# HGRN intra-chunk products by chunk, two tiles to a bank, the neighbour level without an exponential, and eight weight splits on DVE

## The reference, cut to what matters

```python
CHUNK = 64
def step(state, inp):                       # one chunk of 64 tokens
    q_i, k_i, i_i, b_i = inp                # b_i: running sum of log f inside the chunk
    dmat = jnp.exp(jnp.where(causal, b_i[:, :, :, None, :] - b_i[:, :, None, :, :], -jnp.inf))
    attn = jnp.einsum('bhtk,bhsk,bhtsk->bhts', q_i, k_i, dmat)
    o = (jnp.einsum('bhtk,bhkv->bhtv', q_i * jnp.exp(b_i), state)
         + jnp.einsum('bhts,bhsv->bhtv', attn, i_i))
    state = (state * jnp.exp(b_last[:, :, 0, :])[..., None]
             + jnp.einsum('bhsk,bhsv->bhkv', k_i * jnp.exp(b_last - b_i), i_i))
```

## Time and profile before

| | us |
|---|---|
| median of the runs | 1397.89 |
| span of the profiled execution | 1397.8 |
| PE busy in it | 1207.0 |
| DVE busy in it | 753.0 |
| HGRN stage, first product of `hdiag` to first of `hscan` | 329.6 to 422.0 |

### The profile page before, as it was taken

One profiled execution on the slowest core, in us unless ns is written; L12 is line 12 of the kernel. 1 busy time (PEld: TensorE's weight loads), 2 busy tenths in 40 slices (PEclk: granted clock), 3 DMA queues, 4 the chain that ended last, 5 costly groups with the idle time before them and its releaser, 6 DMA issues.

```text
span 1397.8 us, 17492 instructions
## 1 busy us (share of the span) xinstructions
PE 1207.0 (86%) x5935; PEld 983.9 (70%) x5935; DVE 753.0 (54%) x981; ACT 645.5 (46%) x898; POOL 459.8 (33%) x383
## 2 busy tenths in 40 slices
PE   3995899999789965999939999999998995699990
PEld 2775898888678844878828877888777883578770
DVE  4345766536886244999951332242013116499984
ACT  4456333324344232888842233322332323388881
POOL 3343100223222431344453423444231542143332
PEclk9996999999899986999969999999999998699995
DMA  8331100121110355799862322233211345479954
GB/s 228 82 77 37 31 16 16 31 61 45 45 46 16 100 219 173 247 370 368 290 261 87 95 68 84 86 95 98 69 60 46 113 150 220 148 265 368 367 223 198
DMA packets 87131, 195.73 MB, mean 140 GB/s; under 512 B 17372, under 2 KB 18712, under 8 KB 86040
## 3 DMA queue, kind: packets, MB, share of 16 engines
q1 hardware_dynamic: 67992, 161.04, 34.8%
q10 hardware_dynamic: 9280, 17.00, 3.4%
q0 software_dynamic: 9792, 16.80, 3.3%
HBM read 190.61 MB, written 23.07 MB: 153 GB/s over the span
## 4 chain that ended last, share of the span: by engine, by line
PE 67%; DVE 14%; ACT 9%; issue 5%; DMA 3%; POOL 1%; SPq 1%; ACTq 0%; POOLq 0%; DVEq 0%
PE ps L568 17%; PE ps L570 16%; PE ps L569 16%; PE ps L1924 4%; ACT wh L1157 3%; PE ps L2036 2%; ACT hT_hi L1208 2%; PE ps L1807 1%; DVE arena L1518 1%; PE ps L1997 1%; DVE arena L1329 1%; DMA raw<-in_even_w_in_dram 1%; DMA arena<-y 1%; DMA arena<-hs,cur_rows 1%; PE ps L1984 1%
## 5 line engine op out<-in xcount | busy, mean ns | idle before, releaser
L735 POOL TENSOR_TENSOR wl<-raw,wh 128x1024 fp32r<-128x1024 f32 x112 | 271.8, 2434 | 591.4 <-ACT wh L901 591.1
L568 PE MATMUL ps<-wh,hT_hi 128*128 128x512 f32 x928 | 377.7, 407 | 18.9 <-DVE hT_lo L1342 8.1
L570 PE MATMUL ps<-wh,hT_lo 128*128 128x512 f32 x928 | 366.4, 395 | 0.0
L569 PE MATMUL ps<-wl,hT_hi 128*128 128x512 f32 x928 | 366.0, 394 | 0.0
L901 ACT ACTIVATE wh<-raw 128x1024 fp32r<-128x1024 f32 x116 | 122.3, 1059 | 232.1 <-PE ps L570 212.2
L568 PEld LDWEIGHTS ps<-wh,hT_hi 128*128 128x128 f32 x928 | 177.4, 191 | 63.8 <-issue 16.6
L570 PEld LDWEIGHTS ps<-wh,hT_lo 128*128 128x128 f32 x928 | 176.8, 191 | 38.6
L569 PEld LDWEIGHTS ps<-wl,hT_hi 128*128 128x128 f32 x928 | 177.6, 191 | 35.2 <-issue 1.0
L1671 DVE TENSOR_TENSOR wl<-arena,wh 128x1024 fp32r<-128x1024 f32 x96 | 117.6, 1225 | 12.6 <-ACT wh L1157 5.1
L568 PE MATMUL ps<-hT_hi,wh 128*128 128x512 f32 x288 | 116.2, 404 | 9.3 <-DVE hT_lo L1342 8.4
L1671 DVE TENSOR_TENSOR wl<-raw,wh 128x1024 fp32r<-128x1024 f32 x88 | 107.5, 1225 | 17.4 <-ACT wh L901 9.4
(11 more groups left out here) (303 smaller groups left out, 1597.7 us busy)
## 6 DMA issues: line engine op xcount, KB each, us to landing
raw<-in_moe_w_gate_up_dram SPq DMA_DIRECT2D x64, 512.0 KB
arena<-in_moe_w_gate_up_dram SPq DMA_DIRECT2D x64, 512.0 KB, 6.8
raw<-in_odd_w_in_dram SPq DMA_DIRECT2D x48, 512.0 KB
raw<-in_even_w_in_dram SPq DMA_DIRECT2D x32, 512.0 KB
arena<-in_moe_w_down_dram SPq DMA_DIRECT2D x32, 512.0 KB, 7.2
raw<-in_moe_w_down_dram SPq DMA_DIRECT2D x32, 512.0 KB
arena<-y ACTq DMA_DIRECT2D x8, 1024.0 KB, 8.0
raw<-in_odd_w_out_dram SPq DMA_DIRECT2D x16, 512.0 KB
```

Source lines behind the costliest of these rows:

```text
L568: nc.tensor.matmul(dst, lh, rh, start=first, stop=False)
L569: nc.tensor.matmul(dst, lh, rl, start=False, stop=False)
L570: return nc.tensor.matmul(dst, ll, rh, start=False, stop=last)
L735: pool.tensor_tensor(wl[:, i % NSPL, :, :], raw_at(i), wh[:, i % NSPL, :, :].bitcast(F32), ALU.subtract).then_inc(lo_pool, 1)
```

## The change

1. **Products by chunk.** For the diagonal and each level PE makes, instead of 16 products of 128x128x128, 32 of 128x64x64 (128 channels, 64 keys, 64 queries), one for each head and chunk. The even chunk of a tile goes to PSUM partitions 0 to 63, the odd one to 64 to 127, and two tiles of tokens share a bank. `HAT` and the masks have half their width, and DVE reads two banks instead of four with instructions of the same size.
2. **The neighbour level (s = 1).** Its keys have exponent zero and its queries' factor is f = 1 - k. DVE computes (1 - k) q in one instruction during level 4, and no exponents and no exponential are made for it; PE takes k itself as the keys' operand.
3. **Exponentials in halves.** The exponential of a level is taken in two instructions of 1024 elements, each released by its own half of the exponents, and each half's product waits for its own.
4. **Splits.** The remainders of pieces 26 to 33 are written by DVE, at the step of piece i-2, instead of by POOL at the step of piece i-3.
5. **State.** The exponential of b is written over b itself, right after the last of the levels' exponentials, and DVE scales k and q in four tiles each, so that PE's transposes and the scan start with the first.
6. **Constants.** The masks' transfer has half its size, and a 128x64 identity by chunk is made at the start.

```diff
+NEXP = len(LEVELS) - 1
+DVE_LO = range(26, 34)
 def lo_by_dve(i):
-    return any(m + 4 <= i < m + 6 * NE for m in MOE_PIECE)
+    return i in DVE_LO or any(m + 4 <= i < m + 6 * NE for m in MOE_PIECE)
...
-        return [(("lv", step[1], T), "dve") for T in range(NT)]
+        return [(("lv", step[1], pr), "dve") for pr in range(2)]
...
-        lvmask = sb("level_masks", [P, len(LEVELS), P], I8)
+        lvmask = sb("level_masks", [P, len(LEVELS), CH], I8)
+        identc = sb("ident_by_chunk", [P, CH])
...
@@ scalar
             def hgrn(step):
-                n = {"hdiag": 0, "hlevel": step[1] + 1 if len(step) > 1 else 0}.get(step[0])
-                if n is not None:
-                    act.wait_ge(s_("lv_args"), n + 1)
-                    A(act.activation(LE, LE, ACT.Exp), s_("lv_exp"))
+                if step[0] != "hstate":
+                    n = 0 if step[0] == "hdiag" else step[1] + 1
+                    if n < NEXP:
+                        for half in range(2):
+                            e = level_half(LE, n, half)
+                            act.wait_ge(s_("lv_args"), 2 * n + half + 1)
+                            A(act.activation(e, e, ACT.Exp), s_("lv_exp"))
+                    elif n == NEXP:
+                        act.wait_ge(s_("lv_args"), 2 * NEXP + 1)
+                        A(act.activation(LE, LE, ACT.Exp), s_("lv_exp"))
+                        b = HB.rearrange("p h t -> p (h t)")
+                        A(act.activation(b, b, ACT.Exp), s_("lv_exp"))
                 else:
-                    act.wait_ge(s_("hk_decayed"), 1)
-                    A(act.activation(LE, HB.rearrange("p h t -> p (h t)"), ACT.Exp), s_("lv_exp"))
...
@@ vector
                 elif step[0] == "hlevel":
                     n = step[1]
-                    s = LEVELS[n]
-                    e, p_ = halves(LE, s), halves(LP[n % 2], s)
-                    dve.wait_ge(s_("lv_exp"), n + 1)
-                    D(tt(p_[:, :, 0:s], halves(HKf, s)[:, :, 0:s], e[:, :, 0:s], ALU.mult))
-                    D(tt(p_[:, :, s:2 * s], halves(HQf, s)[:, :, s:2 * s], e[:, :, s:2 * s], ALU.mult), s_("lp_ready"))
-                    level_args(n + 1)
+                    if n < NEXP:
+                        for half, src in enumerate((HKf, HQf)):
+                            dve.wait_ge(s_("lv_exp"), 2 * n + half + 1)
+                            D(tt(level_half(LP[n % 2], n, half), level_half(src, n, half), level_half(LE, n, half), ALU.mult), s_("lp_ready"))
+                        if n == NEXP - 1:
+                            odd = [level_half(x, NEXP, 1) for x in (LP[NEXP % 2], HKf, HQf)]
+                            D(stt(odd[0], odd[1], 1.0, odd[2], ALU.subtract, ALU.mult, reverse0=True), s_("lp_ready"))
+                        level_args(n + 1)
-                    for T in range(NT):
-                        tile_is_ready(dve, ("lv", n, T))
-                        D.read(dve.copy_predicated(v3(HAT[:, T, :], 4), bc_m(lvmask[:, n, :]), v3(tile(("lv", n, T)), 4)), ("lv", n, T))
+                    for pr in range(2):
+                        tile_is_ready(dve, ("lv", n, pr))
+                        D.read(dve.copy_predicated(pair_of_hat(pr), bc_m(lvmask[:, n, :], 8), v3(tile(("lv", n, pr)), 8)), ("lv", n, pr))
...
+            def lo(i):
+                dve.wait_ge(hi_done, i + 1)
+                wait_spl_free(dve, i)
+                tt(wl[:, i % NSPL, :, :], raw_at(i), wh[:, i % NSPL, :, :].bitcast(F32), ALU.subtract).then_inc(lo_dve, 1)
...
+                elif k == "piece":
+                    i = first_piece(step[1]) + step[2] + 2
+                    if i in DVE_LO:
+                        lo(i)
...
@@ tensor
+                def by_chunk(name, pr, lhs, rhs):
+                    t = open_tile(name)
+                    for T in (2 * pr, 2 * pr + 1):
+                        for h in range(NH):
+                            for c in range(2):
+                                o, tc = CH * (4 * (T % 2) + h), slice(P * T + CH * c, P * T + CH * c + CH)
+                                ins = mm(t[CH * c:CH * c + CH, o:o + CH], lhs[:, h, tc], rhs[:, h, tc], start=True, stop=True)
+                    done(ins)
...
                 elif step[0] == "hlevel":
-                    pe.wait_ge(s_("lp_ready"), step[1] + 1)
-                    lp = v3(LP[step[1] % 2], 4)
-                    for T in range(NT):
-                        four(("lv", step[1], T), lambda o, h: mm(o, lp[:, h, cols(T)], lp[:, h, cols(T)], start=True, stop=True))
+                    n = step[1]
+                    lp = v3(LP[n % 2], 4)
+                    pe.wait_ge(s_("lp_ready"), 2 * n + 2 if n < NEXP else 2 * NEXP + 1)
+                    for pr in range(2):
+                        by_chunk(("lv", n, pr), pr, lp if n < NEXP else HK, lp)
```

More of the change, by code:

```diff
@@ L272, in side_tiles @@
     if k == "hdiag":
-        return [(("dg", T), "dve") for T in range(NT)]
+        return [(("dg", pr), "dve") for pr in range(2)]
     if k == "hlevel":
-        return [(("lv", step[1], T), "dve") for T in range(NT)]
+        return [(("lv", step[1], pr), "dve") for pr in range(2)]
     if k == "hstate":
@@ new lines, in hgrn @@
+                    for pr in range(2):
+                        tile_is_ready(dve, ("lv", n, pr))
+                        D.read(dve.copy_predicated(pair_of_hat(pr), bc_m(lvmask[:, n, :], 8), v3(tile(("lv", n, pr)), 8)), ("lv", n, pr))
+                elif step[0] == "hstate":
+                    dve.wait_ge(s_("lv_exp"), 2 * NEXP + 1)
+                    for T in range(NT):
+                        D(tt(HK[:, :, cols(T)], HK[:, :, cols(T)], v3(LE, 4)[:, :, cols(T)], ALU.mult), s_("hk_decayed"))
+                    dve.wait_ge(s_("lv_exp"), 2 * NEXP + 2)
+                    for T in range(NT):
+                        D(tt(HQ[:, :, cols(T)], HQ[:, :, cols(T)], HB[:, :, cols(T)], ALU.mult), s_("hq_decayed"))
@@ L2010, in hscan @@
                 for h in range(NH):
[L2011 removed]
+                    mm(t[r, cols(h)], HAT[r, T, h, :], HI[r, T, cols(h)], start=h == 0, stop=False)
                 if c > 0:
```

54 lines of the change are left out of this document (27 added, 27 removed).

## The result

The changed kernel takes 1384.87 us (median, 1382.67 to 1385.93), the one before 1397.81 in the same series: ratio 0.9905, 95% interval 0.9891 to 0.9919, so 12.9 us faster. Forecast were 1391.5, half of that gain; 1385.5 stood there as the first rival.

A forecast was written before the change was run, and what follows sets the result against it. PE was taken as backbone, waiting for DVE in the stage: levels 28.3, pieces 44.6, transposes 1.9, idle 9.4, clock 1.9 make 86.1 against 92.4 us. With 0.2 from the start, the forecast was 1391.5 us, range 1384 to 1398.

The forecast's parts named there:

- first rival: Products alternating between PSUM halves overlap on PE: 30 ns a record, a level 2.1 us, total 1385.5; chance 0.15.
- What bounds the kernel: Whole kernel: PE is the backbone; in the stage PE waits 14.1 us for DVE's products, 20.4 us with the clock.
- the gain passes on to the end: Behind the stage PE has no fixed appointment, so the stage's gain carries to the end one to one.
- PE's records: Diagonal and six levels: 64 records at 60 ns, 4.04 us a level, 0.55 more than before, seven times: +3.9 us.
- The floor of small matmuls: Skill's rule on small products: about 62 ns each with decoder off, 25 ns on; taken to support 60 ns a record.
- DVE: DVE's work in the stage: copies, exponents, products, scaling, splits and POOL collisions sum to -15 of 77 us.
- The splits' share: Eight splits moved to DVE add 10.1 us there, while collisions with POOL go: -12 us.
- ACT: Exponentials in halves: two cost 0.2 us more a level, but the second half's product waits only for its own.
- Neighbour level: Exponents of two halves less on DVE, -2.5 us, and products 12 to 10 and one of another kind, -1.2.
- The path: Stage level by level: PE idle 0.8, 2.1, 0.4, 2.4, 3.7 us, none before level 5, clock 1.9 at level 4; 86.1 us.
- Start: Kernel start: the masks' halved transfer saves 0 to 0.5 us, taken as 0.2.
- Execution and median: Whole time: the profiled execution's span stands 0.1 us from the median, so 1391.4 becomes 1391.5.

The follow-up runs named there:

- e5: Changed kernel with the neighbour level treated as the others again (its exponents, exponential and two products): 1384.07 us, ratio 0.9892 to the kernel before.
- e1: Changed kernel with all even chunks of a bank multiplied first, then all odd ones, same instructions: 1390.96 us, ratio 0.9944 to the kernel before.
- e8: Changed kernel with ACT taking all four silus of block 6 at once, ahead of level 4's exponential: 1381.71 us, ratio 0.9871.
- e3: Kernel before with only the eight splits moved from POOL to DVE: 1395.15 us, ratio 0.9977, stage 88.4 us.
- e2: Changed kernel with all splits of the stage back on POOL: 1391.42 us, ratio 0.9948, stage 84.9 us.
- e4: Changed kernel with one exponential of 2048 elements a level instead of two of 1024: 1386.20 us, ratio 0.9916, stage 83.5 us.
- e7: Changed kernel with the masks' transfer at its old 384 KB: 1383.36 us, ratio 0.9901 to the kernel before.
- e10: e8 with DVE's two scalings and eight gate passes of block 6 moved to where DVE waits for PE: 1389.93 us, ratio 0.9948.
- e11: e10 with the norm's reductions one level later and the splits behind the products: 1387.94 us, ratio 0.9915, stage 64.7 us.
- e15: e12 with two useless DVE instructions of 0.7 us ahead of the scan's chunk 0: 1388.07 us, ratio 0.9905.
- e16: Changed kernel with 7.7 us of useless DVE instructions ahead of the scan's chunk 0: 1406.20 us, ratio 1.0063.
- e13: Changed kernel with 3 us of useless DVE instructions between chunks 0 and 1 of the scan: 1386.31 us, ratio 0.9920.
- e12: e11 with DVE's scaling ahead of the last split and gate passes ahead of and behind chunk 0: 1369.37 us, ratio 0.9803.
- e14: e12 with the norm's second half moved behind level 4 and one tile's gate behind the state's scaling: 1369.78 us, ratio 0.9805.

## Why the prediction was wrong, step by step

- **What bounds the kernel.** Right: PE as backbone of the whole, and DVE's products as its only releaser (14.1 before and after). That the gain passes on to the end held too. Inside the stage DVE is the chain as far as level 4 (e5).
- **PE's records: the step that failed.** "I take 60, the nearest row for a record with few columns." For a record by itself that was nearly right: 58 within one half (e1). What failed is that the forecast added 64 of them one behind the other. Records of the two halves run side by side, which makes 29.6 a record. The row of 20x20 records has no pair in different halves, so it could not speak on this. A level is 2.02 instead of 4.04, 14.1 us less in seven of them. The waits came to 14.1 for 9.4 and the clock to 5.3 for 1.9, so 86.1 - 14.1 + 4.7 + 3.4 = 80.1 stands by the 80.4 measured. With most of the pairs taken away (e1) the stage is 83.2 and the time 1391.0, close to the forecast's 1391.5; the time is partly chance, as the stage was forecast at 86.1.
- **What that gives back.** The first rival had the place (30 ns a record) and the sum: waits 15.9 and clock 3, against 14.1 and 5.3 measured (1.4, 2.3 and 1.6 behind the three waits, with the start of the dense piece), by 80.0 = 7 x 2.02 + 8 x 5.57 + 1.86 + 14.1 + 5.3. Only the last 1.6 lengthens the stage (e5, e8); the rest would have been waits. Its 1385.5 stands 0.6 from the result. The rule of the Trainium skill, "TensorEngine Tiling (Array Packing)", Key Properties, that different tiles load and multiply in parallel, was put beside it with a chance of 0.15; by e1 it holds here for the two column halves. My reason against it was a row that had no two tiles.
- **The floor of small matmuls.** The forecast took 60 ns as the price of a record, whatever it holds. The changed kernel has 29.6 on average and 6 between the two of a pair, so no such price by record binds here. The Trainium skill, "TensorE: Matmul & The Clock Gate", section "Wait — 56ns, not 53.3ns?", gives about 62 ns a product for a decoder that is off; the 29.6 ns a record lie well below that.
- **DVE.** -15 of 77 was right in sum: 62.8 for 76.9. The splits' share was mis-sized. The forecast made it -12 + 10 = -2 us of DVE; in the stage it is 4.0 (e3) to 4.5 (e2). Three of the eight splits stand behind level 4's products, where DVE has time to spare, while three collisions of 2 us each (3.26 and 3.25 for 1.23, 2.74 for 0.69) stood ahead of them. All seven add up to 10.4 us in DVE's timeline of before, not 12.
- **ACT.** "Two halves cost 0.2 more a level" missed that they are worth 3.1 us of stage (e4): the squares and the silus that DVE waits for stand behind the exponentials.
- **Neighbour level.** The saving of 3.7 us in exponents and products was entered in DVE's sum but lies where DVE waits for PE (e5: 0).
- **The path.** Level 5 without a wait: right. Waits of 0.8, 2.1, 0.4, 2.4, 3.7 became 2.58, 2.13, 1.40, 4.36, 3.62; where they grew, PE was free earlier. The clock fell at three levels, not one; at level 4, the one that was forecast, it cost 1.6 for the 1.9.
- **Start.** 0.2 from the masks: not shown (e7).
- **Execution and median.** The forecast set span and median equal (0.1 apart). The executions of both kernels whose span is on record have some 2 us around it, so the span of 1397.8 was hardly of the median execution. The span fell by 14.9 us, the median by 12.9.

## What to carry to other kernels

Products with 64 output partitions are worth giving in alternation to both halves of PSUM: here the same instructions cost 51 or 30 ns on average by the order of a loop alone. And a stretch at the low clock is not yet lost time: where another engine sets the next start, as DVE does for level 1, it only fills a wait (e5). When a wait goes, look whose work stands ahead of it: two table loads and gate passes, which could wait 20 us, were worth more (e8, e10) than the change's own edits on ACT and in the last level. And before trusting a shorter stage, time it often: e10's first execution said 1372, its median 1390.

## What the runs showed that I had not expected

- A wait of about one us at the wrong place costs 14 to 18. In the scan, behind it, the clock stayed at the 1.2 GHz level for 44 us while PE was busy all the time (e11). The other long executions have no profile, but the mean granted clock on record is 0.922 to 0.927 in them and 0.935 to 0.941 in the short ones. With a wait of 1.1 to 1.5 us in chunk 1 behind the short stage 15 of 20 executions were long (e10, e11, e15: 5 of 6, 5 of 6, 5 of 8), with 3.2 us all 6 (e16), with 1.2 us in chunk 2 behind the long stage none of 5 (e13), without it none of 10 (e12, e14), though e14 has one of 2.75 ahead of the scan. What picks the executions is open.
- The length of a wait alone doesn't decide in the levels either: 2.58 us before level 0 is followed by a level of 3.36 us in the changed kernel and of 2.09 in e5, the same instructions.
- An instruction of DVE that ran beside a split of POOL took 3.3 for 1.22 (e2), and ahead of the scan one such collision of 2.2 us was enough for the wait above (e10, e11).
